# Moving the query/key squares and the turned retention output from VectorE to ScalarE, and normalising in six fused products

## The reference

```python
def retention_out(o, z, gn_g):
    of = of * lax.rsqrt(jnp.mean(of * of, axis=-1, keepdims=True) + EPS)
    of = of.reshape(B, T, R_V) * gn_g
    return jax.nn.silu(z) * of
...
qr = rotary(q_r.reshape(B, T, R_HEADS, R_DK), pos) * (R_DK ** -0.5)
kr = rotary(k_r.reshape(B, T, R_HEADS, R_DK), pos)
y_r = retention_out(o_r, z_r, gn_g)
qa = rmsnorm(q_a.reshape(B, T, A_HEADS, A_DH), qn_g)
ka = rmsnorm(k_a.reshape(B, T, A_HEADS, A_DH), kn_g)
y_a, k_rows, v_rows = att_mix(qa, ka, va, rbias)
mixed = jax.nn.sigmoid(m_r) * (y_r @ w_br_ret) + jax.nn.sigmoid(m_a) * (y_a @ w_br_att)
```

## Time and profile before

| what | value |
|---|---|
| median of three runs | 1945.87 us (1944.68 to 1947.09) |
| the profiled execution: its time | 1945.64 us |
| its span, first to last instruction | 1943.9 us |
| mean granted TensorE clock | 0.985 |
| TensorE matmul busy | 1830.5 us (94%) |
| VectorE busy | 985.4 us (51%) |
| ScalarE busy | 737.7 us (38%) |
| GpSimd busy | 355.9 us (18%) |

### The profile page before, as it was taken

The page is one execution under the profiler, slowest core; times in us unless marked ns, Lnnn a source line. Parts: engine busy times, 40 slices in busy tenths (PEclk is TensorE's granted clock), DMA queues, the critical chain, the costliest instruction groups (busy, mean ns, idle before and its releaser), DMA issues.

```text
span 1943.9 us, 34369 instructions
## 1 busy us (share of the span) xinstructions
PE 1830.5 (94%) x11834; PEld 1639.9 (84%) x11834; DVE 985.4 (51%) x1390; ACT 737.7 (38%) x1240; POOL 355.9 (18%) x440
## 2 busy tenths in 40 slices
PE   3799999999999989999989999999999999999998
PEld 2577777777999979999978777777789999899998
DVE  2345555555634366553344555555564334755333
ACT  2243443444523235442223444444453222544322
POOL 1133333333000030000020433333320001200000
PEclk8899999999999999999999999999999999999999
DMA  8286776676555553446536777667647465344442
GB/s 291 75 222 179 188 192 194 187 193 193 188 194 184 166 193 117 122 131 213 169 115 194 194 193 192 187 194 193 193 132 240 159 223 196 98 121 128 130 130 98
DMA packets 444443, 335.44 MB, mean 173 GB/s; under 512 B 150393, under 2 KB 403513, under 8 KB 444354
## 3 DMA queue, kind: packets, MB, share of 16 engines
q1 hardware_dynamic: 429152, 285.40, 50.2%
q0 software_dynamic: 12288, 43.65, 6.7%
q10 hardware_dynamic: 2914, 5.18, 0.7%
HBM read 307.40 MB, written 28.08 MB: 173 GB/s over the span
## 4 chain that ended last, share of the span: by engine, by line
PE 68%; issue 20%; DVE 5%; POOL 3%; DMA 2%; ACT 1%; SPq 0%; POOLq 0%; DVEq 0%; ACTq 0%
PE G L1344 46%; PE G L1368 12%; PE X L1478 6%; PE X L1304 2%; PE X L1391 2%; DVE wlo L925 1%; DMA raw<-in_w_out_dram 1%; DVE qk L1127 1%; POOL small L577 1%; DVE st L1088 1%; ACT prob L714 1%; DMA out_dram<-st 1%; POOL out_dram L503 1%; POOL prob L558 0%; DVE hlo L999 0%
## 5 line engine op out<-in xcount | busy, mean ns | idle before, releaser
L925 DVE TENSOR_TENSOR wlo<-raw,whi 128x1024 fp32r<-128x1024 f32 x369 | 478.8, 1298 | 658.8 <-ACT whi L649 658.0
L649 ACT ACTIVATE whi<-raw 128x1024 fp32r<-128x1024 f32 x369 | 390.9, 1060 | 802.9 <-PE G L1344 438.8
L1368 PE MATMUL G<-whi,hhi 128*128 128x512 f32 x832 | 341.6, 411 | 28.1 <-DVE hlo L999 13.3
L1368 PE MATMUL G<-wlo,hhi 128*128 128x512 f32 x832 | 329.4, 396 | 0.0
L1368 PE MATMUL G<-whi,hlo 128*128 128x512 f32 x832 | 328.8, 395 | 0.0
L1344 PE MATMUL G<-hhi,whi 128*128 128x384 f32 x768 | 261.1, 340 | 6.8 <-DVE hlo L999 6.6
L1344 PE MATMUL G<-hhi,wlo 128*128 128x384 f32 x768 | 257.1, 335 | 0.0
L1344 PE MATMUL G<-hlo,whi 128*128 128x384 f32 x768 | 256.8, 334 | 0.0
L1368 PEld LDWEIGHTS G<-whi,hhi 128*128 128x128 f32 x832 | 159.1, 191 | 77.0 <-issue 31.3
L1344 PE MATMUL G<-ysp,whi 128*128 128x384 f32 x768 | 198.0, 338 | 0.0
L1368 PEld LDWEIGHTS G<-wlo,hhi 128*128 128x128 f32 x832 | 158.8, 191 | 35.4
(11 more groups left out here) (186 smaller groups left out, 2363.4 us busy)
## 6 DMA issues: line engine op xcount, KB each, us to landing
raw<-in_w_in_dram SPq DMA_DIRECT2D x256, 128.0 KB
raw<-in_w_in_dram SPq DMA_DIRECT2D x128, 256.0 KB
ada_w<-in_w_ada_dram SPq DMA_DIRECT2D x64, 512.0 KB, 4.9
raw<-in_w_up_dram SPq DMA_DIRECT2D x64, 512.0 KB
raw<-in_w_down_dram SPq DMA_DIRECT2D x64, 512.0 KB
raw<-in_w_in_dram SPq DMA_DIRECT2D x49, 512.0 KB
kc<-in_cache_attn_k_dram SPq DMA_DIRECT2D x64, 256.0 KB, 5.9
vc<-in_cache_attn_v_dram SPq DMA_DIRECT2D x32, 512.0 KB, 8.4
```

The lines of the kernel that those rows point to most:

```text
L649: return a.activation(out, in_, ACT.Copy)
L925: v.tensor_tensor(wlo[:, j % SPLIT, :, :], raw[:, j % RAW, :, :], whi[:, j % SPLIT, :, :].bitcast(F32), ALU.subtract).then_inc(blk_split, 1)
L1368: ins = t.matmul(B[b][:, :], x[:, kp * WK + k, n * P:(n + 1) * P], w[:, k, :], start=first and k == 0 and x is hhi and w is w_hi, stop=las ...
```

## The change

Three parts. First, the sums of squares of queries and keys are made by ScalarE, with six `Square` activations with an accumulator output, straight from the PSUM accumulators, two ahead of each copy; the wait for `on_ready` protects their target `tq`. VectorE's lines 1121 and 1123 go. Second, the two normalising products over 128x768 become six `scalar_tensor_tensor` operations over 128x128, one for each token tile and each of query and key, that multiply by inverse root and gain at once. Third, `retained` goes from VectorE to ScalarE: there it stands behind `high(5)`, and in the merge one block later, ahead of the branch copies of that block. GpSimd's `rotary` gets one more wait, `orT_done`.

```diff
@@ gpsimd head @@
             pool.wait_ge(tr_done, H)
             pool.wait_ge(kd_ready, H)
+            pool.wait_ge(orT_done, H)
             rotary(c)
-            pool.wait_ge(qk_norm, H + 1)
+            pool.wait_ge(qk_norm, H * 6 + 6)
@@ scalar @@
+        def retained(c, h):
+
+            act.wait_ge(orT_done, c.head)
+            for n in range(2):
+                a.activation(y_ret[:, bass.ds(h * 2 + n, 1), :].rearrange("p a t -> p (a t)"), X[2 * n][:, 0:TOK],
+                             ACT.Identity, scale=gcol[:, n:n + 1]).then_inc(orT_ev, 1)
+
@@ scalar head @@
             act.wait_ge(rope_ready, H)
+            act.wait_ge(on_ready, H)
             for t, e in enumerate(gr[0]):
                 acc(c, e)
+                for r in range(2):
+                    a.activation(tq[:, t, r, :], G[e[0]][:, r * DH:(r + 1) * DH], ACT.Square,
+                                 accum_out=qk_ss[:, 2 * t + r:2 * t + r + 1]).then_inc(qss_ready, 1)
                 copy(qk[:, t, :], G[e[0]][:, :]).then_inc(acc_free[e[0]], 1)
             high(c, 5)
+            if prev is not None:
+                retained(c, prev)
             high(c, 6)
             high(c, 7)
@@ scalar merge @@
                 if first and j == 4:
+                    retained(c, HEADS - 1)
                     branch_high(c, l, 11, 16)
@@ vector head @@
             low(c, 4)
             keys_turned(c, 1)
-            if prev is not None:
-                retained(c, prev)
             low(c, 5)
 
             copied(c, gr[0])
-            q4 = qkA.rearrange("p t (a d) -> p t a d", a=2)
-            c.op(v.tensor_tensor(tq, q4, q4, ALU.mult))
-            c.settle()
-            c.op(v.tensor_reduce(qk_ss.rearrange("p (t a) -> p t a", a=2), tq, axis=AXX, op=ALU.add))
-            c.settle()
+            dve.wait_ge(qss_ready, H * 6 + 6)
             v.tensor_scalar(qk_ms, qk_ss, 1.0 / DH, EPS, ALU.mult, ALU.add).then_inc(qk_msr, 1)
             dve.wait_ge(qk_pow, H + 1)
-            c.op(v.tensor_tensor(q4, q4, qk_rs.rearrange("p (t a) -> p t a", a=2).unsqueeze(3).to_broadcast([P, NT, 2, DH]),
-                                 ALU.mult))
-            c.settle()
-            v.tensor_tensor(qkA, qkA, gqk[:, l:l + 1, :].to_broadcast([P, NT, 2 * DH]), ALU.mult).then_inc(qk_norm, 1)
+            for n in range(2 * NT):
+                part = qk[:, n // 2, n % 2 * DH:(n % 2 + 1) * DH]
+                v.scalar_tensor_tensor(out=part, in0=part, scalar=qk_rs[:, n:n + 1], in1=gqk[:, l, n % 2 * DH:(n % 2 + 1) * DH],
+                                       op0=ALU.mult, op1=ALU.mult).then_inc(qk_norm, 1)
             low(c, 6)
@@ vector merge @@
                 if first and j == 3:
                     branch_low(c, l, 7, 11)
-                    retained(c, HEADS - 1)
@@ tensor head @@
-            pe.wait_ge(qk_norm, H + 1)
+            pe.wait_ge(qk_norm, H * 6 + 6)
             pe.wait_ge(pair_ev, H * 4 + (P0 - 2))
```

More of the change, by code:

```diff
@@ L305, in trunk @@
     va_out, ka_out, st_out, stp_out, y_out = (sem(n) for n in ("va_out", "ka_out", "st_out", "stp_out", "y_out"))
-    qk_msr, qk_pow, qk_norm, ta_done, qa_ev, ka_ev = (
-        sem(n) for n in ("qk_msr", "qk_pow", "qk_norm", "ta_done", "qa_ev", "ka_ev"))
+    qss_ready, qk_msr, qk_pow, qk_norm, ta_done, qa_ev, ka_ev = (
+        sem(n) for n in ("qss_ready", "qk_msr", "qk_pow", "qk_norm", "ta_done", "qa_ev", "ka_ev"))
     sp_done, ss_done, sp_read, ss_read, maxp_ready, maxs_ready, exp_done = (
@@ L1075, in gated @@
                 ins.then_inc(on_ready, 1) if t == NT - 1 else c.op(ins)
[L1077 to L1082, removed]
         def pair(c, q):
```

## The result

| | before | changed |
|---|---|---|
| median | 1945.7 us | 1929.4 us (4 runs, 1929.1 to 1930.7) |
| ratio | | 0.9917, 95% interval 0.9900 to 0.9934 |
| span of the profiled execution | 1943.9 us | 1927.5 us |

What follows compares the result with a forecast made beforehand. TensorE's matmuls fill 94% of the span, so the change counts only where TensorE waits, at the turning. 14 x 1.15 + 2 x 1.4 = 18.9 us on 1945.64 gave 1964.5, so 1965; 8-in-10 range 1934 to 1970.

Steps and rivals of the forecast that it cites:

- the turning: TensorE's turning of `qk` behind `gemm(5)` in 14 looped heads: it waits for the `pair` operations, 2.56 us a head to win.
- ScalarE's two squares: Two 128x128 squares ahead of the last accumulator's copy: 0.26 us each, 0.53 for two, at most 0.74.
- `low(5)` waiting for `high(5)`: On VectorE ahead of the power: `low(5)` starts at 219.07, 0.27 us later than in the kernel before.
- the turned output costing and giving nothing: `retained` on ScalarE: two copies of some 0.4 us behind `high(5)`, done by 220.0, costing nothing.
- the power 1.7 us earlier: GpSimd's power behind VectorE's scale: with two VectorE operations gone, it and `rotary` come 1.71 us forward.
- the fused products in turns of 0.75 us: VectorE's six products beside GpSimd's `rotary`: one waits for one, 0.75 us apart.
- their end where line 1130 ended: The sixth fused product ends at 226.42, line 1130 before at 226.46: the whole gain ahead is eaten up.
- the tie: Behind the sixth product, `low(6)` (226.34) and GpSimd's sum (226.35): turning 0.56 us earlier or 1.15 later, by who goes first.
- What is late next: Step on `low(6)` and GpSimd's sum behind the sixth pair of turns: the sum goes first, turning 1.15 us later.
- GpSimd's win: At the tie: sum to 228.20, `low(6)` to 229.28, turning at 230.65, 1.15 us later a head.
- Rival 1: VectorE wins the tie at `low(6)`: 14 x 0.56 + 2 x 0.34 = 8.5 us less, 1937; chance 0.24.

Runs made afterwards that it cites:

- the squares alone: Kernel before with only the squares moved to ScalarE (two wide products, `retained` on VectorE): 1912.2 us, ratio 0.9828.
- the tie with the fill: Changed kernel with a VectorE fill of 128x1 between the six fused products and `low(6)`: 1931.7 us, ratio 0.9928 to the kernel before.
- the last of the tie's two experiments: Changed kernel with a VectorE maximum over 128x64 between the six fused products and `low(6)`: 1981.6 us, ratio 1.0177 to the kernel before.

## Why the prediction was wrong

Right, nearly to the number: the path and the place (the turning); ScalarE's two squares (0.53 us expected; from 215.85 to 216.37 in the profile after, 0.52); `low(5)` waiting for `high(5)` and the turned output costing and giving nothing, shown by the squares alone; the power 1.7 us earlier; the fused products in turns of 0.75 us; their end where line 1130 ended; and the arithmetic of either outcome of the tie: 0.56 us less a head if VectorE went first (0.62 measured), 1.15 more than before if the sum did (1.08, from 2.79 to 3.87).

**The step that failed is the tie**, in "What is late next": "A VectorE operation that starts as late as GpSimd's has lost each time. So I take GpSimd's win." Every row behind that had GpSimd ahead, by 0.01 or 0.04 us; my own reckoning put `low(6)` ahead by 0.01. I stretched the rows to a case with the other sign. The profile after has `low(6)` ahead, as reckoned, and undisturbed (1.21 us). The runs show VectorE first at this place even where the sum's start stands up to 0.005 us ahead, and the sum first when it leads by 0.12 us. This is the rule that the Trainium skill states (SBUF — State Buffer, Who interferes with whom): whoever starts first has the shared pair for the whole instruction, and the order, not the shape of the operations, decides who is blocked. For clear leads the runs here agree with it: 0.12 us at the sum, 0.04 us where `rotary` starts beside VectorE's products. Within 0.005 us the starts of their rows do not bear it out, for the tie with the fill and the norm stage come out opposite ways.

What decides so near a tie is not shown. At the tie `low(6)` follows another VectorE operation at once and the sum comes behind a wait of 0.08 us; in the norm stage it is GpSimd that goes on at once and VectorE that had waited 1.46 us; no run tests whether that matters. The rows that I had could carry neither outcome: they are rounded to 0.01 us, as much as the lead itself, and that the reckoning had the right sign is partly luck.

**A term was left out**, in the sum and in every rival: the granted clock behind a pause. Rival 1, which came true, stood at 1937 us; 4 falls of 1.6 us that went with the pause, and the 0.06 us a head by which it was mis-sized, make nearly all of the difference to 1929.4. The falls stood in the trace of the kernel before, as 5.7 instead of 4.1 us for the same 18 matmuls in 4 of the 14 looped heads, and I had looked at one head that had none. The term grows where the pause grows: the kernel that I did forecast, made by the last of the tie's two experiments, took 1981.6 us and not 1965, with 14 us more in `gemm(6)` than the kernel before. The range's lower end of 1934 failed by this term alone.

What stays open: what settles a tie of a few thousandths of a microsecond; and why a pause of 2.5 to 2.8 us is followed by a fall in some heads and not in others. The runs show how often, not which.

## What to carry to other kernels

VectorE operations with both inputs in SBUF, beside a GpSimd program that reads SBUF, cost more by their number than by their size: to the start of `low(6)` six of 128 columns took 4.47 us and two of 768 columns 2.83, with GpSimd waiting 1.58 and 1.94. Before splitting or fusing, look at what GpSimd does in the same microseconds, and let it wait if it has time, which here was one line and worth more than the change. The two outcomes of one near tie between two engines lay 52 us apart here, over 2% of the kernel; where a reckoning ends in one, it is an edge to be moved on purpose, not a thing to be forecast. Price a pause of TensorE with the slower products behind it, and look at several turns of a loop for that, not at one.

## What had not been expected of the hardware

Behind a pause of TensorE of 2.17 us, start to start, the granted clock stayed at 2.4 GHz in all 14 looped heads; behind 2.54 us it fell to 1.2 GHz in 2, behind 2.8 in 4, behind 3.9 or more in 12 to 14. Each fall made the next block of 18 matmuls, or it and its neighbours together, 1.6 us longer, so that a pause longer by 0.6 us cost 1.1.

A fill of 128x1 between two VectorE operations moved the second by 0.01 us only; its row stands with a start behind that of the operation that follows it (224.63 and 224.61).
